# Attention with keys first and values divided on tokens, and own places for the halves of the first two blocks of a phase, in a two-layer model on one Trainium2 core

## The reference

```
x = x + pool_mixer(rmsnorm(x)); x = x + conv_ffn(rmsnorm(x))          # phases 0 and 1
x = x + chunk_attention(rmsnorm(x)); x = x + conv_ffn(rmsnorm(x))     # phases 2 and 3
x = x + w_out(sigmoid(ga) * retention + sigmoid(gb) * stick_breaking) # phase 4
x = x + peer(rmsnorm(x))                                              # phase 5, 16384 experts

chunk_attention: q, k, v = split(h @ w_qkv); q, k normed per head of 64 (16 heads)
  s = q k^T / 8 + bias, masked by chunks of 64;  p = softmax(s);  o = p v;  return o @ w_o
conv_ffn: a = causal_conv3(h @ w_gate);  return (silu(a) * (h @ w_val)) @ w_out     # width 2816
```

## Time and profile before

| | |
|---|---|
| median of 3 runs | 1665.75 us (1663.77 to 1665.84) |
| profiled execution | 1667.29 us, its span 1665.5 us |
| mean granted clock of TensorE | 0.994 of 2.4 GHz |
| TensorE busy | 1617.6 us, 97% |
| VectorE busy | 1187.7 us, 71% |
| ScalarE busy | 809.6 us, 49% |
| GpSimd busy | 377.6 us, 23% |
| transfers | 277.75 MB, mean 167 GB/s |

### The profile page before, as it was taken

One profiled execution on the slowest core, in us unless ns is written; L12 is line 12 of the kernel. 1 busy time (PEld: TensorE's weight loads), 2 busy tenths in 40 slices (PEclk: granted clock), 3 DMA queues, 4 the chain that ended last, 5 costly groups with the idle time before them and its releaser, 6 DMA issues.

```text
span 1665.5 us, 29089 instructions
## 1 busy us (share of the span) xinstructions
PE 1617.6 (97%) x11502; PEld 1487.1 (89%) x11502; DVE 1187.7 (71%) x2110; ACT 809.6 (49%) x1559; POOL 377.6 (23%) x252
## 2 busy tenths in 40 slices
PE   6999999899999999999999989999999999999999
PEld 6999986789999878989999989999999888888887
DVE  6766677666666846566778978989999655555555
ACT  6545444645455555443454444444444544444443
POOL 1111135321112201000168762333334000000000
PEclk9999999999999999999999999999999999999999
DMA  5655565346655643435545544445444565555554
GB/s 182 182 181 185 182 196 171 102 140 192 187 180 176 197 154 119 141 122 174 161 153 169 176 160 145 154 154 160 153 152 141 177 190 188 187 186 188 188 188 139
DMA packets 77478, 277.75 MB, mean 167 GB/s; under 512 B 8600, under 2 KB 9880, under 8 KB 77344
## 3 DMA queue, kind: packets, MB, share of 16 engines
q1 hardware_dynamic: 77344, 275.90, 52.6%
HBM read 274.82 MB, written 1.05 MB: 166 GB/s over the span
## 4 chain that ended last, share of the span: by engine, by line
PE 85%; DVE 7%; POOL 3%; ACT 2%; issue 2%; DMA 0%; SPq 0%; ACTq 0%; DVEq 0%; POOLq 0%
PE ps L878 84%; DVE WL L371 2%; POOL WL L371 1%; ACT WH L511 1%; DVE HL L1346 1%; DVE SQN L1343 1%; DVE XT L1343 1%; POOL NR L422 1%; POOL WH L431 0%; PE ps L1032 0%; ACT HH L529 0%; DMA XT<-xt 0%; PE ps L1051 0%; ACT SQN L518 0%; DVE ZS L1346 0%
## 5 line engine op out<-in xcount | busy, mean ns | idle before, releaser
L371 DVE TENSOR_TENSOR WL<-RAW,WH 128x1024 fp32r<-128x1024 f32 x459 | 568.3, 1239 | 239.6 <-ACT WH L511 207.8
L878 PE MATMUL ps<-HH,WH 128*128 128x256 f32 x2016 | 583.4, 289 | 7.2 <-DVE WL L371 2.5
L878 PE MATMUL ps<-HL,WH 128*128 128x256 f32 x2016 | 571.5, 284 | 0.0
L878 PE MATMUL ps<-HH,WL 128*128 128x256 f32 x2016 | 571.2, 283 | 0.0
L511 ACT ACTIVATE WH<-RAW 128x1024 fp32r<-128x1024 f32 x379 | 398.8, 1053 | 246.8 <-PE ps L878 245.7
L878 PEld LDWEIGHTS ps<-HH,WH 128*128 128x128 f32 x2016 | 387.5, 192 | 12.4 <-issue 4.4
L878 PEld LDWEIGHTS ps<-HL,WH 128*128 128x128 f32 x2016 | 387.9, 192 | 1.1 <-issue 1.0
L878 PEld LDWEIGHTS ps<-HH,WL 128*128 128x128 f32 x2016 | 387.7, 192 | 0.0
L431 POOL CAST WH<-RAW 128x1024 fp32r<-128x1024 f32 x127 | 151.7, 1197 | 429.4 <-PE ps L878 429.3
L878 PE MATMUL ps<-WH,GH 128*128 128x512 f32 x512 | 202.6, 396 | 1.8 <-DVE GL L1343 1.8
L878 PE MATMUL ps<-WL,GH 128*128 128x512 f32 x512 | 202.5, 396 | 0.0
(11 more groups left out here) (235 smaller groups left out, 2324.9 us busy)
## 6 DMA issues: line engine op xcount, KB each, us to landing
RAW<-wall SPq DMA_DIRECT2D x510, 512.0 KB, 3.5
B<-rel SPq DMA_DIRECT2D x4, 768.0 KB, 5.4
DEC<-con SPq DMA_DIRECT2D x4, 384.0 KB, 4.4
XT<-xt SPq DMA_DIRECT2D x4, 256.0 KB, 6.0
out<-XT SPq DMA_DIRECT2D x4, 256.0 KB, 2.1
WIN<-con SPq DMA_DIRECT2D x1, 768.0 KB, 9.1
PAR<-par SPq DMA_DIRECT2D x1, 190.0 KB, 2.5
BIG<-keys SPq DMA_DIRECT2D x1, 128.0 KB, 4.5
```

The lines of the kernel that those rows point to most:

```text
L371: ins = eng.tensor_tensor(wl, RAW[:, b % NRAW, :], wh.bitcast(F), ALU.subtract)
L878: return pe.matmul(o, l, r, start=start, stop=stop, skip_group_check=True)
```

## The change

Three things in one. **Attention**: in each half the keys come first (the block order g = 2, 0, 3, 1), so groups 0 and 2 are now keys, scaled on DVE, and groups 1 and 3 queries, squared and copied; the banks, slots and orders go with it, and scores start at slot 10. The division by the sum goes from the 128 x 384 exponentials (weights(m), gone) to the 128 x 64 outputs of each head: turn(m) takes the plain exponentials two slots after the scores, values(m) has PT as the stationary operand and VN moving, so that tokens stand on the partitions; values_normed multiplies four heads with RC at once into NSQ, values_turned transposes back in the same bank, and values_high and values_low take two m at a time. In attention most high halves are made by ACT, eight by POOL. **Own places**: the first two blocks of each phase have places EH and EL, and the ring of three holds the others (halves, wait_place), so the halves of the next phase's first three blocks are made before the phase ends (made_at) in attention and mixer. At odd entries low(b0+1) and low(b0+2) leave enter. **At the start of ffn** conv(0) and silu(0) stand ahead of the halves of block b0+5, and a Silu of one column is run before. NAT and NSQ serve attention and mixer. The routing with four fp32 blocks (DIRECT) stands in both kernels.

```diff
@@ _order, tables of places and slots
-    for g in (0, 2, 1, 3):
+    for g in (2, 0, 3, 1):
         names.extend(("qk", 4 * g + k) for k in range(4))
...
+OWN = {b + i: i for b in ENTRY[1:] for i in range(2)}
+_ring = [b for b in range(N_BLOCKS) if b not in OWN]
+RING = {b: q % NSPLIT for q, b in enumerate(_ring)}
+AFTER = {b: _ring[q - NSPLIT] if q >= NSPLIT else None for q, b in enumerate(_ring)}
+AFTER.update((ENTRY[r] + i, ENTRY[r - 1] + i if r > 1 else None) for r in range(1, 6) for i in range(2))
...
+HIGH_ATT = (13, 14, 16, 17, 22, 23, 25, 26)
...
-    return b in SECOND or ATT + 5 <= b < ENTRY[3] or b - MIX in HIGH_MIX or UP + ROUTED + 4 <= b < WP
+    return b in (SECOND[0], SECOND[1], SECOND[3]) or b - ATT in HIGH_ATT or b - MIX in HIGH_MIX or UP + ROUTED + 4 <= b < WP
...
-NTR_BANK = [(0, 1), (2, 3), (4, 5), (6, 7), (0, 1), (2, 3), (4, 5), (2, 3)]
-
-SCALED = {1: 0, 3: 1, 4: 2, 5: 3}
+NTR_BANK = [(0, 1), (2, 3), (0, 1), (6, 7), (0, 1), (2, 3), (4, 5), (2, 3)]
+
+SCALED = {0: 0, 2: 1, 4: 2, 5: 3}
...
-SCO_SLOT = {12: 0, 13: 1, 15: 2, 16: 3, 19: 4, 20: 5, 22: 6, 23: 7}
-PV_SLOT = {20: (0, 1), 21: (2, 3), 24: (4, 5), 26: (6,), 27: (7,)}
+SCO_SLOT = {10: 0, 11: 1, 13: 2, 14: 3, 19: 4, 20: 5, 22: 6, 23: 7}
+
+PV_SLOT = {20: 0, 21: 1, 24: 2, 26: 3}
+VT_SLOT = {21: 0, 22: 1, 25: 2, 27: 3}
...
+def made_at(b, end):
+
+    return {end - 3: (b + 2, b + 3), end - 2: (b + 3, b + 4)}.get(b, (b + 2,))
...
+        with ExitStack() as sub:
+            EH, EL = sb("EH", [128, 2, BLK], R, sub), sb("EL", [128, 2, BLK], R, sub)
+
+        NAT, NSQ = (sb(n, [128, 2, 2, 512], F, early) for n in ("NAT", "NSQ"))
...
-                ANAT, ASQ = (sb(n, [128, 2, 2, 512], F, sub) for n in ("ANAT", "ASQ"))
...
+        def halves(b):
+
+            if b in OWN:
+                return EH[:, OWN[b], :], EL[:, OWN[b], :]
+            return WH[:, RING[b], :], WL[:, RING[b], :]
+
+        def wait_place(eng, b):
+
+            if AFTER[b] is not None:
+                eng.wait_ge(s_blk, AFTER[b] + 1)
@@ pool_program
             def high(b):
                 pool.wait_ge(d_raw[b % NRAW], 16 * (b // NRAW + 1))
-                pool.wait_ge(s_blk, b - NSPLIT + 1)
-                pool.tensor_copy(WH[:, b % NSPLIT, :], RAW[:, b % NRAW, :]).then_inc(s_hip, 1)
+                wait_place(pool, b)
+                pool.tensor_copy(halves(b)[0], RAW[:, b % NRAW, :]).then_inc(s_hip, 1)
...
-            for n in range(3, 30):
-                high(ATT + n + 2)
-                if n == 5:
+            for n in range(3, 31):
+                if n in (5, 9, 13, 17):
+                    group_power(n // 4 - 1)
+                if n == 10:
                     power(2)
-                if n in (5, 8, 13, 16):
-                    group_power({5: 0, 8: 1, 13: 2, 16: 3}[n])
-            second(3)
+                for b in made_at(ATT + n, ENTRY[3]):
+                    if high_on_pool(b):
+                        high(b)
@@ scalar_program: enter(r) and ffn(l)
                 if r:
-                    high(b0 + 2)
                     high(b0 + 3)
                     high(b0 + 4)
+                if r in (1, 3):
+                    act.activation(WARM[:, :], ONEC[:, :], ACT.Silu)
...
                 conv_now(0)
+                silu(0)
                 high(ENTRY[1 + 2 * l] + 5)
-                silu(0)
                 conv_now(1)
@@ scalar_program: attention
-            def weights(m):
-                act.wait_ge(s_rec, m + 1)
-                for i, (lo, hi) in enumerate(SPANS):
-                    for a in range(2):
-                        c, h = 4 * m + 2 * i + a, 2 * m + a
-                        act.activation(SS[:, h, lo:hi], SS[:, h, lo:hi], ACT.Copy, scale=RC[:, c:c + 1]).then_inc(s_prob, 1)
...
+            def values_high(g):
+                act.wait_ge(s_at, g + 1)
+                act.activation(AH[:, 2 * g:2 * g + 2, :].rearrange("p k t -> p (k t)"), bank[PV_BANK[g]][:, :],
+                               ACT.Copy).then_inc(s_ah, 1)
...
-                if n in (7, 12, 14, 19):
...
+                if n in (9, 10, 18):
+                    for g in {9: (0,), 10: (1,), 18: (2, 3)}[n]:
+                        group_taken(g, (K, Q)[g % 2][:, 4 * (g // 2):4 * (g // 2) + 4, :], ("attn_k_norm", "attn_q_norm")[g % 2])
...
-                if n - 4 in SCO_SLOT:
-                    weights_copied(SCO_SLOT[n - 4])
...
+                if n - 3 in SCO_SLOT:
+                    weights_copied(SCO_SLOT[n - 3])
                 if n in (4, 12):
+                    group_squares(n // 4 - 1, NSQ)
+                for b in made_at(ATT + n, ENTRY[3]):
+                    if not high_on_pool(b):
+                        high(b)
+                if n in (8, 16):
+                    act.wait_ge(s_blk, ATT + NAT_LAST[n // 4 - 1] + 1)
                     group_copied(n // 4 - 1)
+                    group_squares(n // 4 - 1, NSQ)
...
-                if n - 2 in SCO_SLOT:
-                    weights(SCO_SLOT[n - 2])
                 if n - 1 in SCO_SLOT:
                     exps(SCO_SLOT[n - 1])
@@ tensor_program: attention
             def turn(m):
-                pe.wait_ge(s_prob, 4 * m + 4)
-                if m:
+                pe.wait_ge(s_exp, 4 * m + 4)
+                if m == 4:
+                    pe.wait_ge(s_nev, 6)
+                elif m:
                     pe.wait_ge(s_pt, 2 * m)
...
             def values(m):
...
-                    mm(o[r, c:c + T], VN[:, 0, 64 * h:64 * h + 64], PT[:, h, 0:T], True, False)
-                    ins = mm(o[r, c + 128:c + T], VN[:, 1, 64 * h:64 * h + 64], PT[:, h, T:384], False, True)
+                    h, c = 2 * m + a, T * (m % 2) + 64 * a
+                    v0, v1 = (VN[:, t_, 64 * h:64 * h + 64] for t_ in range(2))
+                    mm(o[:, c:c + 64], PT[:, h, 0:128], v0, True, True)
+                    mm(o[:, c + 128:c + 192], PT[:, h, 128:T], v0, True, False)
+                    ins = mm(o[:, c + 128:c + 192], PT[:, h, T:384], v1, False, True)
                 ins.then_inc(s_pv, 1)
+
+            def values_turned(g):
+
+                pe.wait_ge(s_an, g + 1)
+                for i in range(4):
+                    ins = pe.transpose(bank[PV_BANK[g]][:, c128(i)], NSQ[:, 0, g % 2, c128(i)], IDENT)
+                ins.then_inc(s_at, 1)
...
-                if n in (6, 11, 13, 18):
-                    group_turned({6: 0, 11: 1, 13: 2, 18: 3}[n], ANAT)
-                if n - 3 in SCO_SLOT:
-                    turn(SCO_SLOT[n - 3])
+                if n in (8, 9, 17):
+                    for g in {8: (0,), 9: (1,), 17: (2, 3)}[n]:
+                        group_turned(g, NAT)
                 if n in SCO_SLOT:
                     scores(SCO_SLOT[n])
-                for m in PV_SLOT.get(n, ()):
-                    values(m)
+                if n - 2 in SCO_SLOT:
+                    turn(SCO_SLOT[n - 2])
+                if n in VT_SLOT:
+                    values_turned(VT_SLOT[n])
+                if n in PV_SLOT:
+                    values(2 * PV_SLOT[n])
+                    values(2 * PV_SLOT[n] + 1)
@@ vector_program: enter(r), ffn(l), attention
-                if r:
-                    low(dve, b0 + 1)
                 squares_added(r)
...
-                low(dve, b0 + 2)
                 norm_mean(r, bank[7] if r == 5 else bank[0])
...
                 gate(0)
+                conv(0)
                 low(dve, ENTRY[1 + 2 * l] + 5)
-                conv(0)
                 gate(1)
...
+            def values_normed(g):
+
+                dve.wait_ge(s_pv, 2 * g + 2)
+                dve.wait_ge(s_rec, 2 * g + 2)
+                if g >= 2:
+                    dve.wait_ge(s_at, g - 1)
+                tt(heads(NSQ[:, 0, g % 2, :]), heads(bank[PV_BANK[g]][:, :]), RC[:, 8 * g:8 * g + 8].unsqueeze(2).to_broadcast(
+                    [128, 8, 64]), ALU.mult).then_inc(s_an, 1)
...
+                if n in (5, 9, 13, 17):
+                    group_mean(n // 4 - 1, NSQ)
+                if n in (7, 14):
+                    g = 0 if n == 7 else 2
+                    group_root(g)
+                    if g == 2:
+                        dve.wait_ge(s_nt, 2)
+                    group_scaled(g, NAT, natural_banks(g))
+                if n in (10, 18):
+                    group_root((n - 6) // 4, 0.125)
...
+                for b in made_at(ATT + n, ENTRY[3]):
+                    low_if_mine(b)
+                if n == 11:
                     norm_root(2)
```

More of the change, by code:

```diff
@@ L261, in build @@
             CG, SG = (sb(n, [128, 2, 2, 64], F, ph) for n in ("CG", "SG"))
-            SEL1 = sb("SEL1", [8, 512], F, ph)
+            SEL1 = sb("SEL1", [8, 256], F, ph)
             DEC = sb("DEC", [128, 8, 384], F, ph)
-            RQ, RK, SQ, SK = (sb(n, [128, 4, T], F, ph) for n in ("RQ", "RK", "SQ", "SK"))
+            RQ, RK = (sb(n, [128, 4, T], F, ph) for n in ("RQ", "RK"))
             RV, SV = sb("RV", [128, 2, D], F, ph), sb("SV", [128, 2, 512], F, ph)
```

(25 more changed lines are left out.)

112 lines of the change are left out of this document (48 added, 64 removed).

## The result

The changed kernel takes 1655.88 us (median of 4 runs, 1654.20 to 1656.03) against 1665.8 for the kernel before beside it: ratio 0.9939, 95% interval 0.9922 to 0.9956, so 9.9 us or 0.6% less. The profiled execution took 1656.01 us with a span of 1654.2. The sign, the range and the mechanism in attention held; the forecast of 1660.6 was 4.7 us too slow.

The account below looks back on a forecast made before the run. TensorE, busy 97%, was taken as the bound. Attention 4.0 us plus entries 1.2 made 5.2 off the profiled 1667.29, so 1662.1, or 1660.6 on the median's scale (1665.75); range 1655 to 1665.5.

Parts of the forecast that it names:

- Attention, what could be won: Attention phase: TensorE's waits of 10.1 us plus 4.0 us of slow clock, at the utmost 14.1 us to win.
- Added work of TensorE: Attention's values: 96 records at 0.101 us and 16 transposes replace 64 old records, 5.3 us more.
- Rival D: Values matmuls: a 64-column record costs far more than 0.101 us, gain gone from 0.155, 1669.2 at 0.19; chance 0.05.
- turn(3): Attention, after block 16: TensorE waits 2.5 us because VectorE is late and weights_copied(2) stands behind exps(3).
- Rival A: Attention: VectorE keeps up, turn(3) isn't late, clock stays at 2.4 GHz; 4.8 us more gain, 1655.8; chance 0.20.
- Rival B: Attention: the 5.5 us wait returns at group_turned(2) and (3), or own places give nothing; 1663.9; chance 0.25.
- Rival C: Attention: exponentials late at each of the first four turns, 15.6 us in place of 4.8; 1671.4; chance 0.06.
- Sum in attention: Attention in total: 14.1 less 5.3 added work and 4.8 remaining waits and clock, 4.0 us won.
- Entries: Phase entries: 0.65 us won at entry 1, 0.4 at 3, 0.5 at 5, less 0.4 elsewhere; 1.15 in total.
- the 0.4 charged at entries 2 and 4: Entries 2 and 4: GpSimd's earlier cast can fall on FP or FL, 0.2 us lost at each.
- The FL wait: First out block at entries 1 and 3: of the 1.60 us wait for FL, 1.2 kept at entry 1.
- SP's queue, routing, WARM at nothing: SP's loads queue no longer, routing only shifts with entry 5, the Silu table load gives nothing of its own.

Follow-up runs that it names:

- the matmul kernel: Separate kernel of back-to-back matmul rows on TensorE alone, operand distances and column counts varied: 119.9 to 120.0 ns at distances 0 and 128, 117.4 to 118.3 at 32, 64, 96.
- copy_first: The changed kernel with weights_copied(2) ahead of exps(3) on ScalarE: 1653.91 us, ratio 0.9934.
- shift_only: The kernel before plus an unused 4-byte tensor behind ONEC, moving everything allocated behind it by 32 bytes, no instruction changed: 1664.56 us, ratio 0.9996.
- after_no_shift: The changed kernel with WARM as second column of ONEC, so no tensor behind it moves by 32 bytes: 1656.31 us, ratio 0.9945.
- no_own: The changed kernel with all blocks in the ring of three again, casts and low halves of the entries as before: 1658.87 us, ratio 0.9957.
- order_undone: The changed kernel with the sixth block's halves again ahead of silu(0) and conv(0) on ScalarE and VectorE: 1658.73 us, ratio 0.9953.
- weights_64: The changed kernel with WH, WL, EH and EL 64 bytes past a multiple of 128: 1642.51 us, ratio 0.9868.
- the kernel with both edits: The changed kernel with WH, WL, EH, EL 64 bytes past a multiple of 128 and weights_copied(2) ahead of exps(3): 1640.22 us, ratio 0.9838.

## Why the prediction was right or wrong, point by point

- **Bound.** Right: TensorE, and its waits in attention.
- **Attention, what could be won** (14.1 us: 10.1 of waits, 4.0 of clock). Somewhat small. By families of records, natural blocks with the waits and slow spells in them took 81.1 us before and 71.9 after (9.2 less), transposes of groups and weights 10.6 and 9.0 (1.6), the norm's sums 0.8 and 0.4: 11.2 won. By rows, 4.2 stay now (waits of 2.22 and 0.31, and 1.7 of clock), against my 4.8. So the pool was 15.4, not 14.1. Of the 1.3 more, 0.3 is slow clock in the window from 264 to 268 (granted 0.93), which I left out; the rest is in no wait and stays open.
- **Added work of TensorE.** Mechanism right, size small: 10.5 us for the values where I had 9.7 (0.108 a record with 64 columns in three groups and 0.113 in the first, not 0.101), 1.5 for 16 transposes (forecast 1.6): 5.9 against 5.3. The trouble is in the row chosen, but not in its one column: in the matmul kernel 1, 64 and 128 moving columns all take 0.111 to 0.112. Why the eight records of the earlier trace rows were faster stays open. Rival D needed 0.155 and is out. The Trainium skill's figure, "TensorE: Matmul & The Clock Gate", section "Back-to-back issue gap", of about 81 ns a pair at 128 columns is lower still; the measurement decides.
- **turn(3)** waits 2.22 us (forecast 2.5), released as said by the copies behind exps(3); copy_first shows that cause. The second wait I forecast, 0.6 at group_turned(2), didn't come. Rival A fell with this wait, though its time, 1655.8, was hit: the right number for another reason. Rival B fell too: no long wait at group_turned. Rival C: only one of the four turns waited.
- **Sum in attention**: 11.2 - 5.9, and 0.8 from the wo blocks (22.9 us instead of 23.7, most of it placement), is 6.15 against 4.0 forecast, between these two executions. But the 129.17 us of before are one draw: shift_only has the same order of work and the same wait of 2.78 us before a low half, no slow spell behind it, and attention takes 127.36. The forecast charged 1.4 us to that spell and more to the next as if they were fixed. Between shift_only and the changed kernel, with one slow spell each and the same placement of FH and AH, the gain is 4.3; between before and after_no_shift, 7.1. So what attention gained beyond the 4.0 lies within what the clock does from one execution to the next. No run takes the three parts of attention's edit (keys first, division on tokens, high halves on ScalarE) one by one, so how they share the gain is argued from rows, not shown.
- **Entries.** 1.15 forecast, 2.65 measured. Entry 1 gained 1.32 (forecast 0.65: 18.67 us from its first block to the first out block before, 17.35 now), entry 3 0.64 (0.4), entry 5 0.69 (0.5), and the 0.4 charged at entries 2 and 4 didn't come. At entry 1 the order took off 0.3 and own places 1.0 (no_own 18.38, order_undone 17.67), where my 0.65 stood for both together. The waits of 0.52 and 0.31 went at each (no_own brings them back), and XT's first addition at entry 5 stands 2.2 us ahead of the first block instead of 3.3, later by the 1.0 that was forecast. The FL wait is mis-sized: 1.53 stayed where I kept 1.2. The order took off 0.31, and I left out that own places make TensorE arrive sooner and wait 0.24 longer. At entry 2 GpSimd's cast of block b0 + 1 does fall on FP, which takes 0.42 us as ever, and it is over before the first low part of h:
```profile
213.72 1.04 POOL L463 CAST EH<-RAW 128x1024 fp32r<-128x1024 f32 x1
...
213.81 0.42 DVE L1393 TENSOR_TENSOR FP<-FS,ps 128x256 f32<-128x256 f32 x1 [0.63 <-POOL FS L483]
```
By the full block that the Trainium skill describes ("SBUF — State Buffer", section "SBUF: two separate sides") I had it cost up to 1.04. But the section names VectorE instructions with two inputs in SBUF, and FP has one there and one in PSUM, so page and trace agree and my use of it was wrong. I also misread the 0.45 of the earlier trace rows as less than a full block. In the trace of before, the low part of h beside each of the four casts at entries, both of its large inputs in SBUF, ends 0.27 to 0.28 us behind the cast, the later it starts the less it is stretched: 352.23 against 351.95 in the earlier trace rows, and 223.06 against 222.78 here.
```profile
221.74 1.04 POOL L431 CAST WH<-RAW 128x1024 fp32r<-128x1024 f32 x1 [5.88 <-PE ps L878]
...
222.01 1.05 DVE L1346 SCALAR_TENSOR_TENSOR HL<-XT,PAR,HH 128x256 fp32r<-128x256 f32 x1
```
GpSimd's power behind the start of a low half, 3.81 us instead of 2.90, fits as well. With the power started 0.12 us ahead of a low half, as in the changed kernel at 265.66, neither is stretched; by the same section of the Trainium skill the one that starts first has the port for its whole length, and this place doesn't bear that out.
- **SP's queue, routing, WARM at nothing.** WARM was wrong in kind: its instruction is free, its four bytes aren't. The forecast had no term for the address of a tensor: +2.2 in feed-forward, the mixer's 1.0 (shift_only's mixer is as short as the changed kernel's, 254.35 and 254.47 us against 255.3), 0.5 in attention's output blocks, -1.5 in w. It nets to about 2 us by the stages and 1 by the medians, and no view of before would have given it.
- **The whole**: 5.2 forecast, 11.3 between the profiled executions, 9.9 by the medians. The 6.1 beyond the forecast are 2.1 in attention, 1.5 at the entries, 1.8 from placement outside attention (2.2 + 1.0 - 1.4), 1.0 in the routing and -0.3 in the scatter of the start. The routing's 1.0 is not the change's: shift_only, with the old order, has it too (478.3 us from the end of entry 5 to the w stage, as the changed kernel, against 479.3), and before has a slow spell there that is twice as long. What is sure of the miss is the entries and placement; attention's and the routing's parts hang on the clock of single executions.

## What to carry to other kernels

Count the waits one by one, but take a slow spell behind a wait as a chance and not as a fixed price: look at a second trace of the same code before it goes into a sum. Look at the pitch of back-to-back records before looking for waits: in a kernel that is 97% busy, 2 ns on each of the 6144 records with HH or HL moving are 12 us. And when a wait shortens TensorE's way to a chain on another engine, the wait at the end of that chain grows by as much as was not shortened in the chain itself.

## What the runs showed of the hardware that was not expected

- The pitch of fp32r records with 128 stationary and 256 moving columns depends on where the operands lie: in the feed-forward stages 120.0 ns with both at the same phase of 128 bytes, 117.0 to 118.3 with 32 bytes between them, 117.7 or 113.5 with 64. With 512 moving columns: undisturbed natural blocks most often 227, 233 and 229 at 0, 32 and 64; the w stage 232.4 to 234.4. The same addresses don't always give the same pitch: 120.0, 118.5 in the matmul kernel, 117.7 and 113.5 with the weights at 64, and 233.4 and 232.4 for the w stage of weights_64 and of the kernel with both edits.
- The clock behind a wait is not fixed by its length: behind waits of 1.29 to 1.61 us at the first out blocks the clock stayed full; behind 1.84 there was a slow spell in order_undone and in the kernel with both edits, none in weights_64; behind 2.2 before turn(3) there was one in three traces of seven; behind 2.79 there was one in before, none in shift_only (2.78). In the row with one moving column it fell with no wait before it.
- A GpSimd cast holds up a VectorE instruction that starts in its time with two large inputs in SBUF until it is over (four places in before, 0.27 to 0.28 us from the cast's end to the other's), and doesn't hold up one with one input in PSUM (FP, 0.42).
- Why 64 bytes apart has two levels, and why the last row of the matmul kernel lay at 118.5, isn't settled.
